# First attention in pairs of heads on half tiles of TensorE

## Chip, cores and metric

One core of one Trainium2 chip runs the kernel. The metric is the device time of one execution in microseconds (us). TensorE (PE in the profile) multiplies matrices, VectorE (DVE) and ScalarE (ACT) work element by element, GpSimd (POOL) builds some operands and starts a few loads, and SyncE (SP) starts the stream of weights.

## What is computed

The reference runs 256 tokens of width 1024 through two layers and a further block; all in float32. The change touches the attention of the first layer only: 16 heads of width 64 in 4 groups that share keys and values, and for each head three branches over compressed, selected and windowed keys, gated and summed.

```python
s_c = einsum('bqghd,bjgd->bghqj', qb, k_cmp) * scale - slopes * (tf[:, None] - cmp_mid[None, :])
o_c = einsum('bghqj,bjgd->bqghd', p_c, v_cmp)
...
s_s = einsum('bqghd,bgqnd->bghqn', qb, k_s) * scale - slopes * (tf[:, None] - sel_pos)
p_s = masked_softmax(s_s, sel_pos <= t[:, None])
o_s = einsum('bghqn,bgqnd->bqghd', p_s, v_s)
...
s_w = einsum('bqghd,bkgd->bghqk', qb, k_w) * scale - slopes * dist
o_w = einsum('bghqk,bkgd->bqghd', p_w, v_w)
o = gb[..., 0:1] * o_c + gb[..., 1:2] * o_s + gb[..., 2:3] * o_w
```

With 256 tokens every block of keys is selected and the window covers all, so the second and third branch are both causal attention over the same length with their own keys and values.

## The kernel before

Each engine has its own instruction list, written out in order; semaphores tie the lists together. Weights come as 176 units in a stream, double buffered in `raw`, and are split into a high and a low part (`whi`, `wlo`) by ScalarE and VectorE, so that each product is three matmuls. The stream runs ahead until its buffers are full.

The first attention (`attention("nsa")`, on each of TensorE, ScalarE and VectorE) has 32 items. Item i is head `h = i // 2` and query tile `t = i % 2` of 128 queries. By causality tile 0 sees one block of 128 keys and tile 1 two blocks, so an item has two or four transposed blocks (two branches). For each item:

- TensorE, `scores(i)`: for both branches, queries times keys into one bank of four (`acc`). The queries of two heads lie in `qT`, one on rows 0 to 63 and the other on rows 64 to 127; the keys in `kz` are stored twice, with the other half of the rows zero, so that the matmul runs over all 128 rows.
- VectorE, `bias(i)`: adds the slope times the distance (L1475) and finds the negated maximum (L1477). ScalarE: two exponentials with sums (L580). VectorE, `probs(i)`: reciprocal (L1484), gate (L1487), scaling (L1489, two).
- TensorE, `transposes(i)` (L1024) into one of two banks `tp`; ScalarE copies them to `s_pt` in `att`, two deep (L590).
- TensorE, `values(i)`: one matmul of the compressed branch (L1041, 60 rows, 64 columns), then one for each transposed block (L1044, 128 rows, 64 columns), all into 64 partitions of a bank `gub`; the two heads of a pair take the two halves.
- Every fourth item ScalarE takes the finished bank into `hthi` (L558) and VectorE makes the rest in `htlo` (L1504). In both lists this stands three items behind.

TensorE's order is `scores(i+2)`, `transposes(i-1)`, `values(i-2)`. VectorE's is `bias(i)`, `probs(i-1)`, `post(i-3)`; ScalarE's is `post(i-3)`, exponentials of i, copy of i-1. The second attention (`mla`, L1008, L1010) and the third (`diff`) go by the same code with other matmuls. GpSimd loads gain rows into `wide` (L418); until the first attention begins, `wide` holds a bias table.

Of the kernel before, what the change touches and what calls it, by code (L numbers as in the profile page):

```python
# [22 lines left out]
ACT = mybir.ActivationFunctionType  # L23
# [4 lines left out]
P = 128  # L28
T = 256
# [8 lines left out]
H1, G1, DH = 16, 4, 64  # L38
# [109 lines left out]
RD, _at = {}, 0  # L148
# [9 lines left out]
NITEM = {"nsa": 2 * H1, "mla": H2, "diff": 2 * H3}  # L158
LAG = 3

QK3 = {3: ("q3", 0), 4: ("q3", 2), 6: ("k3", 0), 7: ("k3", 2)}

PW1 = [[0, 1, 2], [3, 4, 5], [6, 7, 8], [9, 10, 11], [12, 13], [14, 15]]
# [15 lines left out]
def item_blocks(kind, i):  # L179

    if kind == "nsa":
        return [(b, k) for b in range(2) for k in range(i % 2 + 1)]
    if kind == "mla":
        return [(0, 0), (1, 0), (1, 1)]
    return [(0, 0), (0, 1)]


def build(nc, stream, cols_d, rows_d, wide_d, x_d, const_d, out_d):
    ctx = ExitStack()
    with ctx:  # L190
# [106 lines left out]
        s_sc = att[:, 0:1024].rearrange("p (i b n) -> p i b n", i=2, b=2)  # L297
        s_pr = att[:, 1024:2048].rearrange("p (i b n) -> p i b n", i=2, b=2)
        s_pt = att[:, 2048:3072].rearrange("p (i n) -> p i n", i=2)


        s_ldx, s_ldc, s_ldk, s_ldr = sem("x_loaded"), sem("cols_loaded"), sem("const_loaded"), sem("rows_loaded")
# [77 lines left out]
        @block.gpsimd  # L380
        def _(pool):
            def zero_halves():

                nc.gpsimd.memset(kz[64:128, 0, :, :], 0.0)
                return nc.gpsimd.memset(kz[0:64, 1, :, :], 0.0)

            nc.gpsimd.memset(kcz[64:128, 0, :], 0.0)
            nc.gpsimd.memset(kcz[0:64, 1, :], 0.0)
            zero_halves().then_inc(ev["kz_zeroed"], 1)
            for n in range(7):  # L390
                if n == 0:
                    pool.wait_ge(ev["cm1"], 1)
                if n == 2:
                    pool.wait_ge(s_ldi, 16)
                    pool.wait_ge(s_ldc, 16)
                    pool.wait_ge(s_ol, 16)
                    pool.wait_ge(s_x, 12)

                    dw = cols[:, CO["w_dw"]:CO["w_dw"] + 8 * TAPS].rearrange("p (k c) -> p c k", c=8)
                    for c, k, cnt, part, at in diag_runs:  # L400
                        ins = nc.gpsimd.tensor_tensor(
                            diag[part][:, at:at + cnt, :], ident.unsqueeze(1).to_broadcast([P, cnt, P]),
                            dw[:, c, k:k + cnt].unsqueeze(2).to_broadcast([P, cnt, P]), ALU.mult)
                    ins.then_inc(ev["diagonals_ready"], 1)
                    pool.wait_ge(s_rs, RSTD["n5"] + 1)
                    cnt = TAPS - SPLIT
                    nc.gpsimd.tensor_tensor(
                        diag_shared[:, 0:cnt, :], ident.unsqueeze(1).to_broadcast([P, cnt, P]),
                        dw[:, SHARED, SPLIT:TAPS].unsqueeze(2).to_broadcast([P, cnt, P]), ALU.mult)\
                        .then_inc(ev["diagonals_ready"], 1)  # L410
                if n == 3:
                    pool.wait_ge(s_evd, plan[U_PW2 + 2][3])
                elif n >= 2:
                    k = {2: 0, 4: 1, 5: 2, 6: 3}[n]
                    pool.wait_ge(s_fg, POST_BASE[k] + POST_PIECES[k])
                if n == 4:
                    zero_halves().then_inc(ev["kz_zeroed"], 1)
                pool.dma_start(wide[:, n % 2, :], wide_d[n].partition_broadcast(P)).then_inc(s_ldw[n % 2], 16)  # L418
# [3 lines left out]
        def _(act):  # L422
# [128 lines left out]
            def attention(kind):  # L551
                base, cnt = ITEM0[kind], NITEM[kind]

                def post(i):
                    g = base + i
                    if kind == "nsa" and i % 4 == 3:
                        act.wait_ge(s_pv, g + 1)
                        nc.scalar.activation(hthi[:, i // 4, :], gub[(i // 4) % 2][:, 0:T], ACT.Copy).then_inc(s_oh, 1)  # L558
                    if kind == "mla":
                        act.wait_ge(s_pv, g + 1)  # L560
                        nc.scalar.activation(hthi[:, i, :], gub[i % 2][:, 0:T], ACT.Copy).then_inc(s_oh, 1)
                    if kind == "diff":
                        act.wait_ge(s_pv, g + 1)
                        nc.scalar.activation(diff_o[:, i % 2, (i // 2) * P:(i // 2 + 1) * P], gub[g % 2][:, 0:P], ACT.Copy)
                        at = (i % 2) * H3 + i // 2
                        nc.scalar.activation(xflat[:, i * P:(i + 1) * P], gub[g % 2][:, 0:P], ACT.Square, accum_out=ss[:, at:at + 1])\
                            .then_inc(s_od, 1)
                        if i == cnt - 2:
                            sqrt_table()

                for i in range(cnt + LAG):
                    if i >= LAG:
                        post(i - LAG)
                    g = base + i
                    if i < cnt:
                        act.wait_ge(s_bia, g + 1)
                        act.wait_ge(s_tr, RD[kind] + max(i - 1, 0))
                        nk = P * (i % 2 + 1) if kind == "nsa" else T
                        for b in range(2):
                            ins = nc.scalar.activation(s_pr[:, g % 2, b, 0:nk], s_sc[:, g % 2, b, 0:nk], ACT.Exp,  # L580
                                                       bias=nmax[:, g % 2, b:b + 1],
                                                       accum_out=lsum[:, g % 2, b:b + 1])
                        ins.then_inc(s_exp, 1)
                    if 1 <= i <= cnt:
                        g, r = base + i - 1, RD[kind] + i - 1
                        w = P * len(item_blocks(kind, i - 1))
                        act.wait_ge(s_tr, r + 1)
                        if g >= 2:
                            act.wait_ge(s_pv, g - 1)
                        nc.scalar.activation(s_pt[:, g % 2, 0:w], tp[r % 2][:, 0:w], ACT.Copy).then_inc(s_tf[r % 2], 1)  # L590

            hi_a(0)
            act.wait_ge(s_ldc, 16)
# [230 lines left out]
        def _(pe):  # L824
# [166 lines left out]
            def attention(kind):  # L991
                base, cnt = ITEM0[kind], NITEM[kind]

                def scores(i):
# [1 line left out]
                    if g >= 4:  # L996
                        pe.wait_ge(s_bia, g - 3)
                    b = acc[g % 4]
                    if kind == "nsa":
                        h, t = i // 2, i % 2  # L1000
                        nk = P * (t + 1)
                        for br in range(2):
                            ins = nc.tensor.matmul(b[:, br * T:br * T + nk], qT[:, h // 2, t * P:(t + 1) * P],  # L1003
                                                   kz[:, h % 2, br * G1 + h // 4, 0:nk], start=True, stop=True)
                    elif kind == "mla":
                        o = (i % 2) * ROPE
                        for t in range(NT):
                            nc.tensor.matmul(b[:, t * T:(t + 1) * T], qT[:, i, t * P:(t + 1) * P], kT2[:, i, :],  # L1008
# [19 lines left out]
                def values(i):  # L1028
                    g, r = base + i, RD[kind] + i
                    pe.wait_ge(s_tf[r % 2], r // 2 + 1)  # L1030
                    blocks = item_blocks(kind, i)

                    def pt(j):
                        return s_pt[:, g % 2, j * P:(j + 1) * P]

                    if kind == "nsa":
                        h, t = i // 2, i % 2
                        if i % 4 == 0 and i >= 8:
                            pe.wait_ge(s_ol, i // 4 - 1)
                        out = gub[(h // 2) % 2][(h % 2) * 64:(h % 2 + 1) * 64, t * P:(t + 1) * P]  # L1040
                        nc.tensor.matmul(out, vcmp[:, :], pct[t][:, h, :], start=True, stop=False)  # L1041
                        for j, (br, k) in enumerate(blocks):
                            c = (COL_VS, COL_VW)[br] + (h // 4) * DH
                            ins = nc.tensor.matmul(out, p1[:, k, c:c + DH], pt(j), start=False, stop=j == len(blocks) - 1)  # L1044
                    elif kind == "mla":
                        pe.wait_ge(s_ol, 8 + i - 1)
                        out = gub[i % 2]
                        nc.tensor.matmul(out[:, 0:P], kv[:, 0, i, NOPE:], pt(0), start=True, stop=True)
# [8 lines left out]
                                                   start=k == 0, stop=k == NT - 1)  # L1057
                    ins.then_inc(s_pv, 1)

                scores(0)  # L1060
                scores(1)
                for i in range(cnt + 2):
# [191 lines left out]
        def _(dve):  # L1254
# [202 lines left out]
            def attention(kind):  # L1457
                base, cnt = ITEM0[kind], NITEM[kind]

                def bias(i):  # L1460
                    g, t = base + i, i % 2
                    dve.wait_ge(s_sco, g + 1)
                    if g >= 2:
                        dve.wait_ge(s_exp, g - 1)
# [6 lines left out]
                                                   op0=ALU.mult, op1=ALU.add))  # L1471
                    else:
                        k = KO["causal" if kind == "nsa" else "dist"] + t * T
                        slope = SLOPES1[i // 2] if kind == "nsa" else -SLOPES3[i // 2]
                        own(V.scalar_tensor_tensor(out=out, in0=const[:, k:k + nk].unsqueeze(1).to_broadcast([P, 2, nk]),  # L1475
                                                   scalar=slope, in1=src, op0=ALU.mult, op1=ALU.add))
                    V.tensor_reduce(nmax[:, g % 2, 0:2], out, AX, ALU.max, negate=True).then_inc(s_bia, 1)  # L1477

                def probs(i):
                    g, t = base + i, i % 2  # L1480
                    s = g % 2
                    nk = P * (t + 1) if kind == "nsa" else T
                    dve.wait_ge(s_exp, g + 1)
                    own(V.reciprocal(pw[:, s, 0:2], lsum[:, s, 0:2]))  # L1484
                    if kind == "nsa":
                        h = i // 2
                        own(V.tensor_tensor(pw[:, s, 2:4], pw[:, s, 0:2], gates[:, t, 3 * h + 1:3 * h + 3], ALU.mult))  # L1487
                        for b in range(2):
                            ins = V.tensor_scalar(s_pr[:, s, b, 0:nk], s_pr[:, s, b, 0:nk], pw[:, s, 2 + b:3 + b], None, ALU.mult)  # L1489
# [476 lines left out]
```

## Time and profile before

| | |
|---|---|
| Median of three runs | 1888.21 us (1884.53 to 1888.35) |
| Profiled execution | 1888.43 us, span 1886.6 us |
| TensorE matmul busy | 1729.1 us, 92% of the span |
| VectorE busy | 1229.9 us, 65% |
| ScalarE busy | 817.3 us, 43% |
| DMA | 285.93 MB, mean 152 GB/s |
| Mean granted TensorE clock | 0.96 of full |

The span is the time between the first and the last instruction that the profiler recorded. Shares of busy time are averages over all stages; the change lies in one stage, so the rows further down are of that stage. A matmul in float32 is recorded as two matmuls, each with its weight load (PEld).

### The profile page before, as it was taken

What the parts mean: (1) busy time and instruction counts of PE and PEld (TensorE: products, weight loads), DVE (VectorE), ACT (ScalarE), POOL (GpSimd) and SP (SyncE); (2) the same over time, 40 slices, a digit from 0 to 9 for tenths busy, and PEclk for the clock granted to TensorE, in tenths of its full rate; (3) what the DMA queues carried; (4) which work ended last, traced back from release to release, by engine and by line L of the source; (5) the groups of instructions that cost most, each with busy time, mean ns of one, the idle gap of its engine ahead of it and who ended that gap; (6) DMA issues with size and microseconds to landing.
All of it is one profiled execution on the core that took longest, in us unless ns stands there. A gap on an engine that the chain in (4) does not pass through costs nothing.

```text
span 1886.6 us, 29289 instructions
## 1 busy us (share of the span) xinstructions
PE 1729.1 (92%) x11365; PEld 1591.6 (84%) x11365; DVE 1229.9 (65%) x1751; ACT 817.3 (43%) x1199; POOL 39.3 (2%) x23
## 2 busy tenths in 40 slices
PE   7869999997697999999989869999899989689998
PEld 7857799996577999999988769999899989479997
DVE  4778566666767566666668956565766554866665
ACT  4556444335344333534353054334533344754433
POOL 0000000000005000000000000000000000000000
PEclk9979999998798999999999989999999999889999
DMA  7610345453223545455434034545354545035544
GB/s 265 212 45 1 99 171 198 174 193 102 99 68 133 192 175 200 146 190 198 177 142 161 1 122 168 195 172 200 146 189 178 196 138 178 2 101 202 199 171 162
DMA packets 53291, 285.93 MB, mean 152 GB/s; under 512 B 5872, under 2 KB 6128, under 8 KB 30704
## 3 DMA queue, kind: packets, MB, share of 16 engines
q1 hardware_dynamic: 52224, 281.46, 41.5%
q0 software_dynamic: 1008, 3.67, 0.5%
q8 instruction: 39, 0.64, 0.1%
q14 instruction: 20, 0.16, 0.0%
HBM read 284.05 MB, written 1.05 MB: 151 GB/s over the span
## 4 chain that ended last, share of the span: by engine, by line
PE 82%; DVE 11%; ACT 4%; issue 2%; DMA 0%; DVEq 0%; SPq 0%; ACTq 0%
PE bank L827 18%; PE bank L828 17%; PE bank L829 17%; PE bank L987 9%; PE bank L956 3%; PE bank L958 3%; PE bank L960 3%; DVE proj L1743 3%; PE bank L841 2%; PE bank L1044 1%; PE bank L1003 1%; ACT whi L437 1%; PE bank L1024 1%; DVE nmax L1477 1%; DVE att L1475 1%
## 5 line engine op out<-in xcount | busy, mean ns | idle before, releaser
L827 PE MATMUL bank<-hthi,whi 128*128 128x256 f32 x2144 | 607.9, 284 | 1.9 <-DVE wlo L1274 1.8
L828 PE MATMUL bank<-htlo,whi 128*128 128x256 f32 x2144 | 607.2, 283 | 0.0
L829 PE MATMUL bank<-hthi,wlo 128*128 128x256 f32 x2144 | 607.1, 283 | 0.0
L1268 DVE TENSOR_TENSOR wlo<-raw,whi 128x2048 fp32r<-128x2048 f32 x175 | 401.4, 2294 | 97.5 <-ACT whi L437 97.3
L827 PEld LDWEIGHTS bank<-hthi,whi 128*128 128x128 f32 x2144 | 411.7, 192 | 7.3 <-DVE wlo L1274 2.2
L828 PEld LDWEIGHTS bank<-htlo,whi 128*128 128x128 f32 x2144 | 411.6, 192 | 4.7
L829 PEld LDWEIGHTS bank<-hthi,wlo 128*128 128x128 f32 x2144 | 411.6, 192 | 0.0
L437 ACT ACTIVATE whi<-raw 128x2048 fp32r<-128x2048 f32 x175 | 333.9, 1908 | 34.8 <-PE bank L829 27.3
L509 ACT ACTIVATE tr<-tr 128x256 f32<-128x256 f32 x132 | 55.1, 418 | 657.8 <-DVE tr L1352 657.8
L1352 DVE TENSOR_TENSOR tr<-bank,rb 128x512 f32<-128x512 f32 x132 | 91.2, 691 | 231.8 <-PE bank L829 231.6
L1274 DVE TENSOR_TENSOR wlo<-raw,whi 128x1024 fp32r<-128x1024 f32 x174 | 214.5, 1233 | 25.5 <-ACT whi L445 25.1
L827 PE MATMUL bank<-whi,hthi 128*128 128x384 f32 (+5 forms) x536 | 183.1, 342 | 25.4 <-DVE htlo L1790 6.9
L445 ACT ACTIVATE whi<-raw 128x1024 fp32r<-128x1024 f32 x174 | 181.4, 1043 | 0.4 <-PE bank L829 0.3
L828 PE MATMUL bank<-wlo,hthi 128*128 128x384 f32 (+5 forms) x536 | 179.7, 335 | 0.0
L829 PE MATMUL bank<-whi,htlo 128*128 128x384 f32 (+5 forms) x536 | 179.4, 335 | 0.0
L827 PEld LDWEIGHTS bank<-whi,hthi 128*128 128x128 f32 (+1 forms) x536 | 103.6, 193 | 31.0 <-issue 14.3
L956 PE MATMUL bank<-whi,hidhi 128*128 128x512 f32 x288 | 114.4, 397 | 9.0 <-DVE hidlo L1360 9.0
L958 PE MATMUL bank<-wlo,hidhi 128*128 128x512 f32 x288 | 113.6, 395 | 0.0
L960 PE MATMUL bank<-whi,hidlo 128*128 128x512 f32 x288 | 112.9, 392 | 0.0
L828 PEld LDWEIGHTS bank<-wlo,hthi 128*128 128x128 f32 (+1 forms) x536 | 103.4, 193 | 0.8
L829 PEld LDWEIGHTS bank<-whi,htlo 128*128 128x128 f32 (+1 forms) x536 | 103.2, 192 | 0.9
L1355 DVE TENSOR_TENSOR tr<-tr 128x256 f32<-128x256 f32 x132 | 57.5, 436 | 63.9 <-ACT tr L509 63.9
(241 smaller groups left out, 2088.9 us busy)
## 6 DMA issues: line engine op xcount, KB each, us to landing
raw<-in_stream SPq DMA_DIRECT2D x176, 1024.0 KB, 5.3
raw<-in_stream SPq DMA_DIRECT2D x176, 512.0 KB, 3.5
wide<-in_wide POOLq DMA_DIRECT2D x7, 512.0 KB, 4.1
x<-in_x SPq DMA_DIRECT2D x1, 1024.0 KB, 5.4
out<-x SPq DMA_DIRECT2D x2, 512.0 KB, 2.9
wide<-in_const SPq DMA_DIRECT2D x1, 960.0 KB, 15.5
const<-in_const SPq DMA_DIRECT2D x1, 897.0 KB, 12.7
cols<-in_cols SPq DMA_DIRECT2D x1, 340.0 KB, 7.8
```

What stands on the lines that cost most here:

```text
L437: nc.scalar.activation(whi[:, s, 0:UA], raw[:, s, 0:UA], ACT.Copy).then_inc(s_hia, 1)
L445: nc.scalar.activation(whi[:, s, UA:UNIT], raw[:, s, UA:UNIT], ACT.Copy).then_inc(s_hib, 1)
L827: nc.tensor.matmul(out, whi_, mhi, start=start, stop=False)
L828: nc.tensor.matmul(out, whi_, mlo, start=False, stop=False)
L829: return nc.tensor.matmul(out, wlo_, mhi, start=False, stop=stop)
L956: nc.tensor.matmul(acc[2 * t + j][:, :], hidhi[:, b, lhs], whi[:, s, sl], start=start, stop=False, skip_group_check=True)
L958: nc.tensor.matmul(acc[2 * t + j][:, :], hidhi[:, b, lhs], wlo[:, s, sl], start=False, stop=False, skip_group_check=True)
L960: ins = nc.tensor.matmul(acc[2 * t + j][:, :], hidlo[:, b, lhs], whi[:, s, sl], start=False, stop=stop, skip_group_check=True)
L987: ins = nc.tensor.matmul(acc[2 * t + j][:, :], a[:, 1, lhs], w[:, s, sl], start=False, stop=False, skip_group_check=True)
L1268: V.tensor_tensor(wlo[:, s, 0:UA], raw[:, s, 0:UA], whi[:, s, 0:UA].bitcast(F32), ALU.subtract)\
L1274: V.tensor_tensor(wlo[:, s, UA:UNIT], raw[:, s, UA:UNIT], whi[:, s, UA:UNIT].bitcast(F32), ALU.subtract)\
L1352: V.tensor_tensor(gu[:, j, :].rearrange("p (h n) -> p h n", h=2), gate_up_bank[j], both, ALU.mult)\
```

## The change

Items are numbered anew: item i is head `2 * (i // 4) + i % 2` and tile `(i // 2) % 2`, so that items 2d and 2d+1 are two heads of one tile. TensorE issues scores and values for such a pair at once and alternates between the two heads: scores on rows 0 to 63 and rows 64 to 127 (`qT` and `kz` are cut in half, so the zero halves are no longer multiplied), into two banks; values into partitions 0 to 63 and 64 to 127 of one bank. The transposed probabilities get four buffers, which lie in `wide`; so GpSimd's first two loads into `wide` wait until the attention is over (`s_ol` at 8).

```diff
+def nsa_item(i):
+    return 2 * (i // 4) + i % 2, (i // 2) % 2
...
+        s_pt_nsa = wide[:, :, :].rearrange("p a n -> p (a n)").rearrange("p (i n) -> p i n", i=4)
+        def prob_t(kind, g):
+            return s_pt_nsa[:, g % 4, :] if kind == "nsa" else s_pt[:, g % 2, :]
...
                 if n == 0:
-                    pool.wait_ge(ev["cm1"], 1)
+                    pool.wait_ge(s_ol, 8)
...
-                        if g >= 2:
-                            act.wait_ge(s_pv, g - 1)
-                        nc.scalar.activation(s_pt[:, g % 2, 0:w], tp[r % 2][:, 0:w], ACT.Copy).then_inc(s_tf[r % 2], 1)
+                        deep = 4 if kind == "nsa" else 2
+                        if g >= deep:
+                            act.wait_ge(s_pv, g - deep + 1)
+                        nc.scalar.activation(prob_t(kind, g)[:, 0:w], tp[r % 2][:, 0:w], ACT.Copy).then_inc(s_tf[r % 2], 1)
...
+                def nsa_scores(d):
+                    i = 2 * d
+                    g = base + i
+                    if g >= 4:
+                        pe.wait_ge(s_bia, g - 2)
+                    c, t = nsa_item(i)[0] // 2, nsa_item(i)[1]
+                    nk = P * (t + 1)
+                    for br in range(2):
+                        for m in range(2):
+                            half = slice(64 * m, 64 * m + 64)
+                            ins = nc.tensor.matmul(acc[(g + m) % 4][:, br * T:br * T + nk], qT[half, c, t * P:(t + 1) * P],
+                                                   kz[half, m, br * G1 + c // 2, 0:nk], start=True, stop=True)
+                            if br == 1:
+                                ins.then_inc(s_sco, 1)
+
+                def nsa_values(d):
+                    i = 2 * d
+                    g, r = base + i, RD[kind] + i
+                    for m in range(2):
+                        pe.wait_ge(s_tf[(r + m) % 2], (r + m) // 2 + 1)
+                    c, t = nsa_item(i)[0] // 2, nsa_item(i)[1]
+                    if t == 0 and c >= 2:
+                        pe.wait_ge(s_ol, c - 1)
+                    out = [gub[c % 2][64 * m:64 * m + 64, t * P:(t + 1) * P] for m in range(2)]
+                    for m in range(2):
+                        nc.tensor.matmul(out[m], vcmp[:, :], pct[t][:, 2 * c + m, :], start=True, stop=False)
+                    blocks = item_blocks(kind, i)
+                    for j, (br, k) in enumerate(blocks):
+                        at = (COL_VS, COL_VW)[br] + (c // 2) * DH
+                        for m in range(2):
+                            ins = nc.tensor.matmul(out[m], p1[:, k, at:at + DH], prob_t(kind, g + m)[:, j * P:(j + 1) * P],
+                                                   start=False, stop=j == len(blocks) - 1)
+                            if j == len(blocks) - 1:
+                                ins.then_inc(s_pv, 1)
+
+                if kind == "nsa":
+                    nsa_scores(0)
+                    for d in range(cnt // 2 + 1):
+                        if d + 1 < cnt // 2:
+                            nsa_scores(d + 1)
+                        for i in (2 * d - 1, 2 * d):
+                            if 0 <= i < cnt:
+                                transposes(i)
+                        if d >= 1:
+                            nsa_values(d - 1)
+                    return
```

TensorE's list in the middle of the first attention, before the change: two items, with the scores (L1003) of the item two ahead. The last number of a row is how many such instructions follow each other.

```order
L1003 MATMUL bank<-tr 128x128 [waits scores_biased]
L1003 MATMUL bank<-tr 128x128
L1024 MATMUL bank<-const,att 128x128 [waits transpose_bank_taken_1,probs_done]
L1024 MATMUL bank<-const,att 128x128 x3
L1041 MATMUL bank<-xn,vcmp 64x128 [waits output_lo_done,transpose_bank_taken_0]
L1044 MATMUL bank<-att,proj 64x128 x2
L1003 MATMUL bank<-tr 128x256 [waits scores_biased]
L1003 MATMUL bank<-tr 128x256
L1024 MATMUL bank<-const,att 128x128 [waits transpose_bank_taken_0,probs_done]
L1024 MATMUL bank<-const,att 128x128
L1041 MATMUL bank<-tr,vcmp 64x128 [waits transpose_bank_taken_1]
L1044 MATMUL bank<-att,proj 64x128 x4
```

The same place after the change; L1065 are the scores of a pair, L1028 the transposes, L1081 and L1086 the values of a pair.

```order
L1065 MATMUL bank<-tr 128x256 [waits scores_biased]
L1065 MATMUL bank<-tr 128x256 x3
L1028 MATMUL bank<-const,att 128x128 [waits transpose_bank_taken_1,probs_done]
L1028 MATMUL bank<-const,att 128x128 x3
L1028 MATMUL bank<-const,att 128x128 [waits transpose_bank_taken_0,probs_done]
L1028 MATMUL bank<-const,att 128x128
L1081 MATMUL bank<-tr,vcmp 64x128 [waits transpose_bank_taken_1,transpose_bank_taken_0]
L1081 MATMUL bank<-tr,vcmp 64x128
L1086 MATMUL bank<-wide,proj 64x128 x8
```

Where one item's scores, the transposes and the values of one item took turns, the transposes of two items now stand together, between the scores of one pair and the values of another.

GpSimd's list around its first loads, before:

```order
L384 MEMSET tr 64x2048
L385 MEMSET tr 64x2048
L418 DMA wide<-in_wide 128x1024 [waits cm1]
L418 DMA wide<-in_wide 128x1024
L401 TENSOR_TENSOR tr<-const,cols 128x3968 [waits output_lo_done,x_updated,cols_loaded,identity_loaded]
```

And after the change:

```order
L393 MEMSET tr 64x2048
L394 MEMSET tr 64x2048
L427 DMA wide<-in_wide 128x1024 [waits output_lo_done]
L427 DMA wide<-in_wide 128x1024
L410 TENSOR_TENSOR tr<-const,cols 128x3968 [waits output_lo_done,x_updated,cols_loaded,identity_loaded]
```

The order stays; the first load waits for the last `htlo` of the attention and no longer for an event ahead of it.

## Rows read from the trace of the kernel before

**Rows 1.** Windows, the first attention: length, busy time of each engine, clock, DMA share, GB/s.
```profile
core 0: us, PE busy (x) PEld busy (x) DVE busy (x) ACT busy (x) POOL busy (x), PEclk, DMA share, GB/s
128.40:210.30 81.90, 77.58 (x481) 56.29 (x481) 61.80 (x200) 47.92 (x169) 0.00 (x0) 0.98 0.00 1
```

**Rows 2.** Chain that ended last, 158.6 to 163: start, length, what.
```profile
158.40 0.36 PE bank L1041 x2
158.76 0.58 PE bank L1044 x4
159.34 1.06 PE bank L1003 x4
160.40 0.22 PE bank L1024 x2
...
160.98 1.02 PE bank L1044 x8
162.00 0.64 PE bank L1003 x4
162.64 0.44 PE bank L1024 x4
```

**Rows 3.** Timeline, 160.5 to 165.1, TensorE and ScalarE: start, length, what, idle before.
```profile
160.91 0.85 PEld L1044 LDWEIGHTS bank<-att,proj 128*64 128x64 f32 x8 [0.17 <-issue]
162.04 0.38 ACT L558 ACTIVATE hthi<-bank 128x256 fp32r<-128x256 f32 x1 [0.99 <-PE bank L1044]
163.11 0.60 ACT L590 ACTIVATE att<-bank 128x512 f32<-128x512 f32 x1
...
165.03 0.44 PE L1024 MATMUL bank<-const,att 128*128 128x128 f32 x2
```

**Rows 4.** Timeline, VectorE, first attention.
```profile
143.41 0.42 DVE L1504 TENSOR_TENSOR htlo<-bank,hthi 128x256 fp32r<-128x256 f32 x1 [1.39 <-ACT hthi L558]
...
162.45 0.42 DVE L1504 TENSOR_TENSOR htlo<-bank,hthi 128x256 fp32r<-128x256 f32 x1 [1.39 <-ACT hthi L558]
162.79 0.68 DVE L1475 SCALAR_TENSOR_TENSOR att<-const,bank 128x512 f32<-128x512 f32 x1
...
164.11 0.15 DVE L1484 RECIPROCAL pw<-lsum 128x2 f32<-128x2 f32 x1
...
164.49 0.48 DVE L1489 TENSOR_SCALAR att<-att,pw 128x128 f32<-128x128 f32 x2
164.89 0.41 DVE L1475 SCALAR_TENSOR_TENSOR att<-const,bank 128x256 f32<-128x256 f32 x1
...
165.67 0.15 DVE L1484 RECIPROCAL pw<-lsum 128x2 f32<-128x2 f32 x1
...
166.59 0.68 DVE L1475 SCALAR_TENSOR_TENSOR att<-const,bank 128x512 f32<-128x512 f32 x1
...
200.53 0.42 DVE L1504 TENSOR_TENSOR htlo<-bank,hthi 128x256 fp32r<-128x256 f32 x1 [1.39 <-ACT hthi L558]
```

**Rows 5.** Chain that ended last, second attention.
```profile
526.87 0.43 PE bank L1008 x2
527.30 0.63 PE bank L1010 x2
```

**Rows 6.** The tile wide, GpSimd's timeline, window and waits behind the attention.
```profile
117.33 1.20 POOL L418 DMA_DIRECT2D wide<-in_wide  x2 [112.58 <-DVE proj L1608]
...
L1386 DVE SCALAR_TENSOR_TENSOR xn<-bank,wide x16: 678/691/692, 963.9 to 1879.7; 128x512 f32<-128x512 f32 x16
...
209.50:240.00 30.50, 27.57 (x185) 27.17 (x186) 16.36 (x21) 14.48 (x17) 0.00 (x0) 1.00 0.49 156
...
ACT whi L437 <- PE bank L829: 13.1, 3, 5.2
```

**Rows 7.** Windows, end of the first attention and middle of the third.
```profile
200.00:204.00 4.00, 2.49 (x17) 1.57 (x17) 2.92 (x10) 3.11 (x11) 0.00 (x0) 1.00 0.00 0
204.00:208.00 4.00, 4.00 (x19) 2.69 (x19) 0.44 (x2) 0.60 (x1) 0.00 (x0) 0.57 0.00 0
...
1620.00:1625.00 5.00, 3.66 (x23) 2.73 (x22) 4.79 (x14) 3.94 (x18) 0.00 (x0) 1.00 0.00 0
```

More of the change, by code:

```diff
@@ L181, in item_blocks @@
     if kind == "nsa":
-        return [(b, k) for b in range(2) for k in range(i % 2 + 1)]
+        return [(b, k) for b in range(2) for k in range(nsa_item(i)[1] + 1)]
     if kind == "mla":
@@ L577, in attention @@
                         act.wait_ge(s_tr, RD[kind] + max(i - 1, 0))
-                        nk = P * (i % 2 + 1) if kind == "nsa" else T
+                        nk = P * (nsa_item(i)[1] + 1) if kind == "nsa" else T
                         for b in range(2):
@@ L998, in scores @@
                     b = acc[g % 4]
[L999 to L1005, printed above, removed]
+                    if kind == "mla":
                         o = (i % 2) * ROPE
@@ L1030, in values @@
                     pe.wait_ge(s_tf[r % 2], r // 2 + 1)
-                    blocks = item_blocks(kind, i)
                     def pt(j):
[L1034 to L1045, printed above, removed]
+                        return prob_t(kind, g)[:, j * P:(j + 1) * P]
+                    if kind == "mla":
                         pe.wait_ge(s_ol, 8 + i - 1)
@@ L1460, in bias @@
                 def bias(i):
-                    g, t = base + i, i % 2
+                    g = base + i
+                    h, t = nsa_item(i) if kind == "nsa" else (i // 2, i % 2)
                     dve.wait_ge(s_sco, g + 1)
@@ L1473, in bias @@
                         k = KO["causal" if kind == "nsa" else "dist"] + t * T
-                        slope = SLOPES1[i // 2] if kind == "nsa" else -SLOPES3[i // 2]
+                        slope = SLOPES1[h] if kind == "nsa" else -SLOPES3[h]
                         own(V.scalar_tensor_tensor(out=out, in0=const[:, k:k + nk].unsqueeze(1).to_broadcast([P, 2, nk]),
@@ L1479, in probs @@
                 def probs(i):
-                    g, t = base + i, i % 2
+                    g = base + i
+                    h, t = nsa_item(i) if kind == "nsa" else (i // 2, i % 2)
                     s = g % 2
@@ L1485, in probs @@
                     if kind == "nsa":
-                        h = i // 2
                         own(V.tensor_tensor(pw[:, s, 2:4], pw[:, s, 0:2], gates[:, t, 3 * h + 1:3 * h + 3], ALU.mult))
```

## Prediction

> **What bounds the kernel now.** I read the windows of the first attention first. The profile's slices are 47 us wide and hide it; the stage is the 81.9 us from 128.4, with TensorE busy 77.58, VectorE 61.80, ScalarE 47.92, and DMA share 0.00 [rows 1]. So no transfer matters inside it, and TensorE or something it waits for sets the pace. Next the chain of waits in one stretch: it never leaves TensorE, piece after piece [rows 2]. The timeline of VectorE and ScalarE then shows how near the next limit is: VectorE works without a gap from 162.79 to 166.59 and waits 1.39 us only before L1504, once in four items [rows 3, 4]. L1504 starts at 143.41 and at 200.53, six periods apart [rows 4]: one group of four items (two heads, two query tiles) takes 9.52 us, and there are eight groups. A saving of 0.47 us per group is a bound of what can be measured: I call 0.2% of the kernel, 3.8 us, the least that can be told from no change.
>
> **What a matmul costs here.** A float32 matmul is two records, which I call passes. Pieces of the chain that differ only in count give the prices. Transposes, no change of tile shape before them: 4 in 0.44, so 0.11 per 128-column pass. L1044: 8 in 1.02 and 4 in 0.58, so 0.14 plus 0.11 each. L1041: 0.36, again 0.14 + 0.22. L1003: 0.64 and 1.06 for 4, so 0.20 plus four of 0.11 or 0.215 [rows 2]. The 0.14 or 0.20 is the change of tile shape: in the second attention L1008 takes 0.43 behind L1024, which has its shape, and the 64-row L1010 behind it 0.63 [rows 5]. A 64-row pass is thus no cheaper by itself: 256 columns take 0.215 on either shape. Whatever the change gains must come from passes on two tiles running together, and that no row of before shows.
>
> **The change part by part.**
> *Work.* The multiplications stay: 128 passes of scores, 64 of L1041, 192 of L1044, 96 transposes, and the same VectorE and ScalarE instructions. Scores get 64-row tiles, so a new change of shape stands between scores and transposes (0.20, the price of L1010), but all changes are now made once per pair: before three per item, six per pair (two each of 0.20, 0.14, 0.14, so 0.96), now four (0.68). That is 0.28 less TensorE work per pair, 0.56 per group, and 4.5 us over the stage if TensorE stayed the only limit.
> *Overlap.* Passes of one tile must follow each other. With instructions alternating A, B, A, B and two passes in each, three answers are possible. Together in full: K alternating instructions cost K pass times. Started in program order: B's first pass may start with A's second and not before, and so on, K+1 pass times. Not at all: 2K. I take the middle: all passes of before stand in the order of the program and the two passes of one instruction stand together, and nothing I see lets B's first overtake A's second. The Trainium skill (TensorE: Matmul & The Clock Gate, Part 3, packing small matmuls) says that matmuls on several tiles start about 4 ns apart but start and end strictly in program order; the trace of before has no pair of tiles to test it on. By that rule the sum is the K+1 one; its measured packs, each with one pass per tile, would alone give the full one.
> *The new cycle.* The changed TensorE order is scores of pair d+1, transposes 2d-1 and 2d, values of pair d-1. Transpose 2d-1 is now queued behind a whole pair's values and scores though its probabilities are ready earlier; behind it wait ScalarE's copy, then the values. I play one group through from L1504 (all times from [rows 2 to 5]):
> VectorE: L1504 to the next start 0.34, bias of a two-block item 1.32 (162.79 to 164.11), its probabilities 0.92 (165.67 to 166.59), and 0.14 until the transposes start (164.89 to 165.03): 2.72 [rows 3, 4].
> TensorE: transposes 0.44; then, with changes of shape 0.14, 0.14, 0.20, 0.20, the vcmp pair, values of a one-block pair, scores of a two-block pair, transposes 0.44.
> ScalarE copies the block: 0.25 from the end of its passes (160.91 + 0.88 of values to 162.04 shows that hop), 0.60 (163.11), and 0.08 back to TensorE, which no row shows where it binds and which I put near VectorE's 0.06 to TensorE (164.97 to 165.03): 0.93.
> TensorE: 0.14, vcmp pair, 0.14, values of the two-block pair. Then 0.25, L558 0.38, 0.03 to L1504: 0.66 [rows 3].
> Fixed part: 2.72 + 0.88 + 0.96 + 0.93 + 0.66 = 6.15. Passes on the cycle, in units of 0.11: started in order 3 + 5 + 10 (scores, five of double width) + 3 + 9 = 30, so 3.30 and a period of **9.45**. In full 24, so 8.79; not at all 48, so 11.43. Even with 9.52 lies at 30.6 passes. So TensorE's own work falls from about 9.36 per group (two times 4.68, the pieces of [rows 2] with L1041's 0.36 counted twice) to about 6.5, and the time hardly moves, since the chain now goes round through VectorE and ScalarE and TensorE stands idle for 3 us of it: what is saved is given back as waits for transposes 2d-1 and for L558. Sum: 8 x (9.45 - 9.52) = -0.6 us.
> *Scores of a one-block pair* are eight weight loads for eight passes; should loads not run together they stay at 0.88 and not 0.55. They lie off the cycle, in TensorE's idle time: nothing. Were that cover gone: 8 x 0.33 = 2.6 us.
> *Four transposed buffers.* With two the copy of an item waited for the values of the item two before, which the pair order issues later; four remove that wait. The copies keep their size and place on ScalarE. Nothing.
> *Loads of wide.* Both move from 117.33 [rows 6] to the end of the attention, as GpSimd now waits for the last L1504. Behind them in its queue stand the diagonals, which wait for later events anyway, and the first reader of these rows, L1386, starts at 963.9 [rows 6]. They land beside the weight stream, at a DMA share of 0.49, where no compute instruction waits for a load [rows 6]. Nothing; if they pushed a weight load into the open it is their own time, about 5 us.
> *Item order* on VectorE changes slopes and widths, not instructions. Nothing.
> The profiled run has 1888.43 us with a span of 1886.6; the median of the three runs is 1888.21. From the median: **1887.6**.
>
> **Rivals.**
> *Full overlap.* 8 x (8.79 - 9.52) = -5.8 us: 1882.4. For it: the tiles share no rows or no columns, and VectorE (about 8.0 per group: twice 3.80 and 0.42) leaves room. Against it: the two passes of each matmul stand together. The Trainium skill (TensorEngine Tiling, Theoretical Speedup) has up to 2x for dimensions of 64 or less, which would be this case; nothing in before shows it.
> *Tiles do not run together: slower.* One place, the alternating passes. If only scores fail, 36 passes, 10.11, +4.7 us: 1892.9. If only values fail (both tiles read the same 128 rows), 42 passes, 10.77, +10 us: 1898. If both, 11.43, +15.3 us: 1903.5. It decides from 31 passes on, for then the pair order only makes later items wait. For it: before shows not one overlap, and a float32 pass already takes some 260 clocks of 2.4 GHz for 128 columns, so it may be bound by something the tiles share. Against it: different rows or columns of the array.
> *The clock falls.* TensorE now waits several times in each group. Before, the granted clock stayed 1.00 through the third attention, with TensorE busy 3.66 of 5 us, but it was 0.57 in 204 to 208, after a stretch of 4 us in which TensorE was busy for 2.49 [rows 7]: part of that time went at 1.2 GHz and not 2.4. Such a dip doubles the passes for about 4 us, some 2 us more on a cycle of which passes are a third to a half. One in every second group: +8 us, 1896. Against it: the waits in the third attention are as long together, if more even.
>
> **How the numbers follow.** Order-bound overlap 0.38 (its own range 1884 to 1891: a change of shape 0.05 dearer or cheaper moves it by 6 x 8 x 0.05 = 2.4), full overlap 0.28, tiles not together 0.20, clock 0.14. Faster by over 0.2%: nearly all of full, a tenth of the first and little else, 0.34. Within: 0.33. Slower: 0.33. The range 1881 to 1897 leaves out values or both serial (0.12), heavy dips (0.04), and more than full overlap (0.03).
>
> **What would show it.** Starts of the post line (L1504 of before) 9.45 apart, with VectorE still waiting at it, say half a microsecond, and TensorE idle before transposes. Passes of a pair: the score piece of four instructions 1.28 with its change of shape (full 1.06, none 1.92), the two-block values 1.13 (full 1.02, none 1.90). Four changes of shape per pair of 0.14 to 0.20. Granted clock 1.00 in every group. It is wrong if the periods are near 8.8, near 10 or more, or if the clock dips; and if the stage is as forecast but the rest moved, the loads of wide are to be looked at.

## The result and the profile after

The changed kernel takes 1892.74 us (median of 11 runs, 1889.92 to 1897.67), the kernel before 1887.2 us (11 runs): ratio 1.0037, 95% interval 1.0025 to 1.005. It is slower by 5.5 us between the medians, where the prediction had no change and gave slower 0.33. The profiled execution is one of the longer ones, 1897.16 us with a span of 1895.4, so 8.8 us over the span of before.

The answer to [rows 1] and [rows 7]: windows of the profile after, in the middle of the first attention; then single groups of four items, from one post line to the next. Columns as in [rows 1]; the ninth is the granted clock.

```profile
144.00:200.00 56.00, 41.86 (x326) 27.84 (x324) 44.08 (x144) 32.09 (x119) 0.00 (x0) 0.81 0.01 1
...
153.60:162.20 8.60, 6.07 (x62) 4.14 (x60) 7.63 (x25) 5.62 (x22) 0.00 (x0) 1.00 0.01 4
162.20:174.40 12.20, 9.66 (x60) 6.46 (x59) 7.80 (x25) 5.76 (x23) 0.00 (x0) 0.63 0.00 0
184.30:193.00 8.70, 6.17 (x64) 4.14 (x60) 7.71 (x25) 5.72 (x22) 0.00 (x0) 1.00 0.00 0
```

Two of these groups have the full clock and take 8.7 us, less than the 9.52 of before; one has 0.63 and takes 12.2. VectorE's busy time is the same in all, TensorE's is not: the same passes are slower.

The answer to [rows 4]: VectorE's timeline after, the post line (L1547, L1504 of before), with what it waited.

```profile
143.67 0.42 DVE L1547 TENSOR_TENSOR htlo<-bank,hthi 128x256 fp32r<-128x256 f32 x1 [0.41 <-ACT hthi L567]
153.54 0.42 DVE L1547 TENSOR_TENSOR htlo<-bank,hthi 128x256 fp32r<-128x256 f32 x1 [0.42 <-ACT hthi L567]
162.24 0.42 DVE L1547 TENSOR_TENSOR htlo<-bank,hthi 128x256 fp32r<-128x256 f32 x1 [0.42 <-ACT hthi L567]
174.41 0.42 DVE L1547 TENSOR_TENSOR htlo<-bank,hthi 128x256 fp32r<-128x256 f32 x1 [1.55 <-ACT hthi L567]
184.30 0.42 DVE L1547 TENSOR_TENSOR htlo<-bank,hthi 128x256 fp32r<-128x256 f32 x1 [0.42 <-ACT hthi L567]
193.00 0.42 DVE L1547 TENSOR_TENSOR htlo<-bank,hthi 128x256 fp32r<-128x256 f32 x1 [0.41 <-ACT hthi L567]
205.20 0.42 DVE L1547 TENSOR_TENSOR htlo<-bank,hthi 128x256 fp32r<-128x256 f32 x1 [1.55 <-ACT hthi L567]
215.62 0.42 DVE L1547 TENSOR_TENSOR htlo<-bank,hthi 128x256 fp32r<-128x256 f32 x1 [6.50 <-ACT hthi L567]
```

The groups take 9.87, 8.70, 12.17, 9.89, 8.70, 12.20 and 10.42 us. The 0.42 us of waiting at the post line, forecast as half a microsecond, is there whenever the clock is full.

The answer to [rows 2]: the chain of waits after, first at the full clock, then at half. L1081 and L1086 are a pair's values, L1065 a pair's scores, L1028 transposes.

```profile
156.25 0.66 PE bank L1028 x4
156.91 0.37 PE bank L1081 x4
157.27 0.59 PE bank L1086 x8
157.86 1.06 PE bank L1065 x8
158.93 0.60 PE bank L1028 x4
...
160.29 0.44 PE bank L1081 x4
160.73 1.07 PE bank L1086 x16
...
164.96 0.86 PE bank L1028 x4
165.82 0.62 PE bank L1081 x4
166.44 1.05 PE bank L1086 x8
167.49 2.01 PE bank L1065 x8
169.50 1.06 PE bank L1028 x4
...
171.32 0.69 PE bank L1081 x4
172.01 1.95 PE bank L1086 x16
```

Eight score passes of 256 columns take 1.06 us, as long as four did before in [rows 2]; sixteen passes of values take 1.07, and eight took 1.02. Two tiles run together almost without loss. In the next group, at half clock, the same scores take 2.01.

These pieces also account for the long group. From 153.54 to 162.24, at the full clock, TensorE's seven pieces on the chain add up to 4.79 us; from 162.24 to 174.41 the same seven add up to 8.24. The difference, 3.45 us, is all but 0.02 of what this group takes more (12.17 against 8.70).

TensorE's timeline after, a wait that stands before a dip of the clock. The same wait of 2.19 us stands before 156.25 and 187.01 too, where the clock stays full:

```profile
193.09 0.44 PE L1028 MATMUL bank<-const,att 128*128 128x128 f32 x2
195.72 0.90 PE L1028 MATMUL bank<-const,att 128*128 128x128 f32 x4 [2.19 <-DVE att L1532]
...
198.22 2.08 PE L1065 MATMUL bank<-tr 64*128 64x256 f32 x8
```

The 8.8 us between the spans come together by landmarks: the first scores start 1.2 us earlier (127.29 against 128.50); from there to the first post line 16.4 against 14.9 us (+1.5, clock 0.68 over 128 to 144 against 1.00); six groups 61.5 against 57.1 (+4.4); the last group 10.4 against 9.3 (+1.1); from the last post line to the first down projection in the loop (L987 before, L997 after) 51.0 against 47.7 (+3.3: the clock is still at half when the next stage begins, see the third line); and the rest of the kernel is 0.3 us shorter.

```profile
128.00:144.00 16.00, 11.70 (x81) 7.74 (x77) 12.20 (x39) 8.37 (x32) 0.00 (x0) 0.68 0.00 1
...
200.00:216.00 16.00, 11.41 (x70) 7.65 (x68) 6.06 (x18) 6.36 (x20) 0.00 (x0) 0.50 0.00 0
216.00:232.00 16.00, 15.90 (x82) 15.91 (x83) 7.91 (x7) 6.26 (x5) 1.20 (x2) 0.88 0.60 199
```

So the theory for the experiments: the pairs save what full overlap gives, TensorE then waits for VectorE, and the clock falls and takes back more. The rivals: the pair order itself makes some groups long and the clock only goes along; the loads of wide cost something; four buffers do nothing.

### The profile page after: what moved, and what is told of

It is laid out like the page before. It is cut to its first block, busy times and chain, and to the rows that moved or that the text cites. A ratio compares the mean times of both kernels' runs of the same rounds, so it can differ in the third digit from the quotient of the medians.

```text
span 1895.4 us, 29297 instructions
## 1 busy us (share of the span) xinstructions
PE 1719.5 (91%) x11365; PEld 1581.7 (83%) x11365; DVE 1230.6 (65%) x1751; ACT 817.5 (43%) x1199; POOL 39.3 (2%) x23
## 4 chain that ended last, share of the span: by engine, by line
PE 80%; DVE 12%; ACT 5%; issue 2%; DMA 0%; DVEq 0%; SPq 0%; ACTq 0%
PE bank L837 18%; PE bank L839 17%; PE bank L838 17%; PE bank L997 9%; PE bank L966 3%; PE bank L968 3%; PE bank L970 3%; DVE proj L1786 3%; PE bank L851 2%; PE bank L1028 1%; PE bank L1086 1%; DVE nmax L1520 1%; DVE att L1518 1%; ACT whi L446 1%; DVE x L1450 1%
```

## Experiments

All ratios are against the kernel before, run on the same chip in turn. Differences in us between two changed kernels can lie across chips; the kernel before had medians of 1886.83 to 1887.45 us on them, so 0.6 us of such a difference says nothing.

**e1_fill4: something to do in the longest wait.** Ahead of the transposes of item 2d in every second pair stand four matmuls whose result the transposes overwrite.

```diff
                         for i in (2 * d - 1, 2 * d):
+                            if i == 2 * d and d % 2 == 1 and 2 * d < cnt:
+                                bank_free(RD[kind] + i)
+                                for _ in range(4):
+                                    nc.tensor.matmul(tp[(RD[kind] + i) % 2][:, 0:T], qT[:, 0, 0:P], kz[:, 0, 0, :],
+                                                     start=True, stop=True)
                             if 0 <= i < cnt:
                                 transposes(i)
```

> The changed kernel, with four extra 128-row matmuls of 256 columns (their result is overwritten) in TensorE's longest wait of each group, ahead of the transposes of every second pair; 32 extra matmuls, the output unchanged. Theory (clock): the pairs are right and only the granted clock makes the change slower. Then the clock stays near 1.00 in the stage, every group takes 8.7 to 8.8 us, and the kernel is 5 to 7 us faster than before (ratio about 0.997). Rival (pair order): the longer groups come from the queue order itself, the clock is a bystander; then 1.7 us of extra work per group changes nothing or adds up to 1.7 us per group, ratio 1.003 to 1.010.

Measured: 1880.43 us, ratio 0.9961 (0.9948 to 0.9975), so 12.3 us less than the change without them and 6.8 less than before, though TensorE does more. The clock window, VectorE's post line (now L1552) and TensorE's filled wait (L1100):

```profile
144.00:200.00 56.00, 50.17 (x424) 35.10 (x424) 49.56 (x161) 36.96 (x137) 0.00 (x0) 1.00 0.01 1
```

```profile
144.06 0.42 DVE L1552 TENSOR_TENSOR htlo<-bank,hthi 128x256 fp32r<-128x256 f32 x1 [0.42 <-ACT hthi L567]
...
196.26 0.42 DVE L1552 TENSOR_TENSOR htlo<-bank,hthi 128x256 fp32r<-128x256 f32 x1 [0.42 <-ACT hthi L567]
...
161.82 1.89 PE L1100 MATMUL bank<-tr 128*128 128x256 f32 x8
...
164.18 0.66 PE L1028 MATMUL bank<-const,att 128*128 128x128 f32 x4 [0.46 <-DVE att L1537]
```

Six periods in 52.20 us: each 8.70, at a clock of 1.00. That is also what the groups at the full clock take in the change without filling, so the extra matmuls shorten a group in no other way. The order of the pairs makes no group long; the clock theory holds. The filling does not reach the start of the stage: over 128 to 144 the clock is 0.79 here too, and from the first scores to the first post line it takes 16.1 us (14.9 before).

**e2_fill2: half as much.** The same with `range(2)`.

> The same with two extra matmuls in place of four, half the filling (0.86 us per group). Clock theory: fewer dips than the changed kernel, more or as many as with four; ratio between 0.997 and 1.003. Pair order: like the changed kernel, about 1.004.

Measured: 1884.04 us, ratio 0.9982 (0.9967 to 0.9997), between the two. In its profile the clock is 0.91 over 144 to 200, with groups of 8.70 four times, and of 9.97 and 10.83 once each. Half the filling gives fewer dips, not none. TensorE's wait ahead of the transposes is 1.32 us in five of the six groups here, against 2.19 us in the change and 0.46 in e1.

**e3_serial and e10_serial_fill: one head after the other.**

```diff
-                    for br in range(2):
-                        for m in range(2):
+                    for m in range(2):
+                        for br in range(2):
...
-                    for j, (br, k) in enumerate(blocks):
...
-                        for m in range(2):
+                    for m in range(2):
+                        for j, (br, k) in enumerate(blocks):
```

> The changed kernel, but scores and values of a pair are issued one head after the other and not in turns. Theory (tiles run together only when instructions take turns): a two-block score pair takes 1.92 and not 1.06 us, two-block values about 1.9 and not 1.05; groups of 11.4 us by my cycle, at a clock near 1.00 since TensorE is busier; +15 us, ratio 1.008. Rival (each tile has a queue of its own, the order within the pair is all the same): 1.06 and 1.05 us, ratio 1.004 as the change.

Measured: 1900.63 us, ratio 1.0074 (1.0054 to 1.0093), near the number of the first theory but not for its reason: the clock is 0.79 over 144 to 200, and scores take 2.02 us at half clock, as in turns. So the kernel was run again with the filling of e1.

> e3_serial with the four extra matmuls of e1_fill4. In e3_serial two-block values took 1.52 us at the full clock, against 1.07 in turns and 1.88 without any overlap, one-block values 0.81 against 0.59; scores showed no loss at the half clock. With the clock held: scores again 1.06, values 1.52 and 0.81, so the group is 8.70 + 0.45 + 0.22 = about 9.4 us and the kernel near that of before, ratio 0.999 to 1.001. If scores lose too (1.9), groups of 10.2 us and ratio 1.004.

Measured: 1886.41 us, ratio 0.9994 (0.9985 to 1.0004), clock 1.00 over 144 to 200, every group 9.17 us. Its chain of waits:

```profile
167.41 1.07 PE bank L1065 x8
...
170.28 1.52 PE bank L1086 x16
```

Scores lose nothing without taking turns, one-block values nothing (0.59), two-block values 0.45: the group is 8.70 + 0.45 = 9.15. I had added 0.22 for the one-block values from a piece of e3 that lay in a change of clock. In these three cases turns matter only for the longest row, eight passes of 128 columns on each tile; why, no run shows.

**e4_scores128 and e9_scores128_fill: scores over all 128 rows again.**

```diff
-                            ins = nc.tensor.matmul(acc[(g + m) % 4][:, br * T:br * T + nk], qT[half, c, t * P:(t + 1) * P],
-                                                   kz[half, m, br * G1 + c // 2, 0:nk], start=True, stop=True)
+                            ins = nc.tensor.matmul(acc[(g + m) % 4][:, br * T:br * T + nk], qT[:, c, t * P:(t + 1) * P],
+                                                   kz[:, m, br * G1 + c // 2, 0:nk], start=True, stop=True)
```

> The changed kernel, but scores run over all 128 rows with the zero halves, as before; values still alternate. Cycle with full overlap of values only: 24 passes become 32, 8.79 becomes 9.67 us, less the change of shape between scores and transposes (0.20): 9.47. Clock theory: TensorE is busier by 0.88 + 0.44 us per group, so fewer dips than the changed kernel, and the time is about that of before (ratio 0.999 to 1.003) although more work is done. Pair order without the clock: the lost overlap adds its 0.7 us to each group of the changed kernel, ratio about 1.007.

Measured: 1907.41 us, ratio 1.0099 (1.0079 to 1.012). Both expectations missed: TensorE has more to do and the clock is lower still, 0.79 over 144 to 200, with groups of 11.0 to 12.6 us. More work in the busy places does not hold the clock; a wait of 1.90 us still stands ahead of the transposes in every group. With the filling:

> e4_scores128 with the four extra matmuls of e1_fill4. With the clock held the group is 8.70 + 0.86 (eight more score passes on the cycle, of double width, in units of 0.11: 0.88) - 0.20 (no change of shape): about 9.4 to 9.6 us, so +6 us against e1_fill4, ratio 0.999 to 1.001. Rival (128-row scores cost more than their passes, since e4_scores128 was 15 us over the change): 10 us and more, ratio 1.003 or more.

Measured: 1884.98 us, ratio 0.999 (0.998 to 0.9999), clock 1.00 over 144 to 200, groups of 9.41 us.

```profile
165.01 1.92 PE bank L1065 x8
166.94 0.45 PE bank L1028 x4
```

Scores take 1.92 (1.06 on two tiles), and the transposes behind them no longer pay 0.15 for the change of shape (0.45 against 0.60). The half tiles of the scores are worth 0.71 us per group (0.86 less 0.15), within what was expected (9.4 to 9.6 for the group).

**e5_two_deep_fill: transposed probabilities two deep.** Filled as e1; `deep = 2`, the old buffers, the loads of wide at their old time.

> The changed kernel with the four extra matmuls per group (e1_fill4), but transposed probabilities two deep in their old place, and the loads of wide at their old time. Theory (depth matters once the clock holds): the copy of an item waits for values that the pair order issues late; groups of about 9.2 us instead of 8.7, so about 4 us more than e1_fill4, ratio 0.998. Rival (depth is cover only): 8.7 us and ratio 0.996.

Measured: 1886.23 us, ratio 0.9994 (0.9985 to 1.0003), clock 1.00 over 144 to 200, groups of 9.35 us. Expected were about 9.2 and 4 us more than e1; it is 5.8 us more. ScalarE's copies now wait 1.29 and 1.54 us for values (L1086), as the theory says. Without the four buffers the pairs gain 0.17 us per group over the 9.52 of before; the buffers bring the other 0.65. This run also puts the loads of wide back; the next one finds no cost of theirs.

**e6_wide_late: the kernel before with the loads of wide moved.**

```diff
-                    pool.wait_ge(ev["cm1"], 1)
+                    pool.wait_ge(s_ol, 8)
```

> The kernel before, with only GpSimd's first loads into wide moved behind the attention, as the change does. Theory (costs nothing): ratio 1.000, groups of 9.52 us. Rival (the 1 MB beside the weight stream delays a weight load after the attention): 2 to 5 us slower, with a wait for a load between 210 and 230 us.

Measured: 1885.29 us, ratio 0.9993 (0.998 to 1.0005), groups of 9.52, and 47.7 us from the last post line to the first down projection in the loop, as before. No cost of theirs shows.

**e8_tr_first_fill and e7_tr_first: another order.** Item 2d-1 is transposed ahead of the scores of pair d+1; three extra matmuls, then none.

```diff
-                        if d + 1 < cnt // 2:
-                            nsa_scores(d + 1)
                         for i in (2 * d - 1, 2 * d):
+                            if i == 2 * d and d + 1 < cnt // 2:
+                                nsa_scores(d + 1)
```

> The changed kernel with transposes 2d-1 ahead of the scores of pair d+1 and not behind them, and three extra matmuls per group in the wait ahead of transposes 2d. If the cycle is what I drew with full overlap (scores and their change of shape lie on it before transposes 2d-1), the group loses part of them: about 8.5 us against 8.70, so 1 to 2 us less than e1_fill4, ratio about 0.995, clock 1.00. Rival (VectorE already sets the group at 8.7): no change against e1_fill4.

Measured: 1880.15 us, ratio 0.9961 (0.9949 to 0.9974); groups of 8.39 us at a clock of 1.00, and the post line waits for nothing:

```profile
149.71 0.43 DVE L1552 TENSOR_TENSOR htlo<-bank,hthi 128x256 fp32r<-128x256 f32 x1
158.09 0.42 DVE L1552 TENSOR_TENSOR htlo<-bank,hthi 128x256 fp32r<-128x256 f32 x1
166.48 0.42 DVE L1552 TENSOR_TENSOR htlo<-bank,hthi 128x256 fp32r<-128x256 f32 x1
```

The group is shorter by 0.31, which over eight groups is 2.5 us; the medians of this kernel and e1 are 0.3 us apart, so whether it is faster than e1, as expected, is not settled. The rival, that VectorE sets the group at 8.7, is out. Both beat the kernel before and the change.

> e8_tr_first_fill without the extra matmuls: transposes 2d-1 ahead of the scores of pair d+1. If the clock hangs on TensorE's waits, as the runs with filling say, the groups at the full clock take 8.39 us as there, but the clock dips again (below 0.9 over 144 to 200), and the kernel is slower than e8_tr_first_fill by 3 to 10 us. Rival (it was the long waits at one place, and the shorter group has none of them): clock 1.00 and ratio 0.995 to 0.997 with no extra work.

Measured: 1893.78 us, ratio 1.0042 (1.0026 to 1.0058), 13.6 us more than with filling. The clock is 0.79 over 144 to 200; two groups take 8.39, the others 11.1 to 11.3. The dips came as expected, but they cost more than the 3 to 10 us that were put on them.

## Why the prediction was wrong

Two steps failed, and they pull in opposite directions. The overlap of two tiles was sized too small, which put the saving at 0.6 us, where e1, with the clock held, is 6.8 us faster than before; and the main sum kept the granted clock at 1.00, that is, the clock's term at nothing, where the falling clock costs 12.3 us. The second alone turned the change into a slower kernel. Both signs of being wrong that the prediction named have shown themselves: periods near 8.8 us, and a clock that dips.

**What bounds the kernel, the stage and its 9.52 us:** right; e6, which has the order of before, shows 9.52 again.

**Prices of passes and of changes of shape:** right. The pieces forecast for full overlap, scores of 1.06 and two-block values of 1.02, were measured as 1.06 and 1.07; without overlap 1.92 was forecast for scores and e9 shows it.

**"Started in program order ... K+1 pass times. I take the middle": this step failed.** The passes of two tiles run together almost in full, although the two passes of a float32 matmul stand together in the list. Even in e10, with all passes of one head first, scores take 1.07, and in its trace the eight passes start in four pairs, 0.012 to 0.014 us apart within a pair: the second head does not wait for the first. The rule of the Trainium skill (TensorE: Matmul & The Clock Gate, Part 3, packing small matmuls), that matmuls start and end strictly in program order, would have given 1.28; the measurement decides against my sum from it. The rival of full overlap (0.28) had a group of 8.79 and 1882.4 us; with the clock held the group is 8.70 and e1 shows 1880.43.

**"Granted clock 1.00 in every group": this step failed too, and it set the sign.** The mechanism was named, as the rival "the clock falls" (0.14), but its chance was too low and its price as well: one dip in every second group, each 4 us long and 2 us dear, on top of a sum with no saving. Measured, against 8.70 per group, the six groups between the first and the last post line but one lose 1.17, 0, 3.47, 1.19, 0 and 3.50 us, and the dips reach beyond the stage on both sides (+1.5 and +3.3 us against before). In runs, the change without filling is 12.3 us above e1. What was sized wrong is how long the clock stays down. The prediction has four dips of 4 us, 16 us in all; the clock windows above give about 51 us at half clock (10 over 128 to 144, 21 over 144 to 200, 20 behind 200). The one around the 12.17 us group lasts some 10 us, not 4:

```profile
166.00:175.00 9.00, 8.65 (x54) 5.91 (x52) 4.84 (x16) 3.86 (x15) 0.00 (x0) 0.50 0.00 0
```

Per us at half clock the prediction was not too cheap: it took 2 us for 4, and this one lost 3.47 us for 10. What I held against the rival, that the third attention waits as long at a clock of 1.00 [rows 7], was true of sums (idle for 1.34 of 5 us there, for 2.53 of 8.70 us here). But there it is in short waits, of 0.67 us each, and here one wait of 2.19 us stands in five of the six groups (1.45 in the sixth):

```profile
1621.34 0.44 PE L1024 MATMUL bank<-const,att 128*128 128x128 f32 x2 [0.67 <-DVE att L1496]
```

**The cycle worked:** right as a shape. With 24 passes it gave 8.79 (8.70 measured), and the expectation of e9, which stands on it, 9.4 to 9.6 (9.41). It foresaw TensorE's idle time, 3 us per group (2.53 measured at the full clock), but used it only as cover for other terms; by the runs with filling, this idle time is what the clock hangs on.

**Four buffers at nothing:** as put, right, since they remove a wait that the pair order brings; e5 gives that wait a size, 0.65 us per group. **Loads of wide at nothing:** right, by e6. **Item order on VectorE:** its busy time per group at full clock is 7.6 to 7.7 us (7.71 before); I saw no cost.

**The range** of 1881 to 1897 holds 1892.74, but that is partly luck: two errors of opposite sign cancel in part. The time is also next to the 1892.9 of the rival in which the scores do not run together, and e1 and e10 show that they do. The chances did not lean to slower.

Open: what exactly of the waits makes the clock fall. One profile each of e2 and e5 makes a pair to start from: over 144 to 200 TensorE is busy for much the same time in both (46.41 and 46.63 of 56 us), and the clock is 0.91 in e2, whose longest wait is 1.33 us, and 1.00 in e5, whose longest is 0.77. That filling them restores it is shown four times (e1 against the change, e10 against e3, e9 against e4, e8 against e7: 12 to 22 us each); no run varies the length of a wait by itself.

## What to carry to other kernels

Where TensorE sets the pace and is made faster, it begins to wait for the next engine, and its clock may fall: look at the granted clock of the stage and at single periods, not at the mean, before judging the order of instructions. A run with throw-away matmuls in the longest wait tells the two apart, and here it is the faster kernel too. Half tiles ran together almost in full here, for matmuls of 64 rows and for those of 64 columns; most of the gain needed buffers behind them that are deep enough for the pair.

## What the runs showed of the hardware

- Two 64-row or two 64-column tiles run together almost without loss in float32: 8 passes of 256 columns in 1.06 us with the change of shape (4 in 1.06 before), 16 of 128 columns in 1.07 (8 in 1.02 before).
- Taking turns is hardly needed (e10): one head after the other, 8 score passes in 1.07, 8 passes of values in 0.59, and only 16 in 1.52 instead of 1.07.
- In the change the granted clock is 0.81 over a stretch in which TensorE is busy for 41.86 of 56 us and no wait is above 2.2 us; in e1 it stays at 1.00 with 50.17 of 56 us, in e4 it is 0.79 with 44.27.
- At half clock the pieces on the chain take 8.24 us where they take 4.79 at the full clock, and VectorE's busy time per group stays the same (7.80 against 7.63 us).
